# A two-block network on one core: layer norms and residuals of the second block worked one row tile at a time

## The reference, cut to what matters

```python
for layer in range(2):
    mix = even_mixer(x, ...) if layer == 0 else odd_mixer(x, ...)
    x = layer_norm(ALPHA * x + mix, ln1_g, ln1_b)
    x = layer_norm(ALPHA * x + memory_cross_attention(x, mem, xq, xkv, xo), ln2_g, ln2_b)
    x = layer_norm(ALPHA * x + grouped_moe(x, router_w, ...), ln3_g, ln3_b)
```

## Time and profile before

| what | us |
|---|---|
| median of 3 runs | 2657.65 (2654.42 to 2660.9) |
| the profiled execution, its own time | 2666.19 |
| its span, first to last instruction | 2664.3 |
| PE busy | 2455.5 (92%) |
| DVE busy | 1676.5 (63%) |
| ACT busy | 1171.9 (44%) |
| GpSimd busy | 105.5 (4%) |

### The profile page before, as it was taken

How to read it: one execution, slowest core, us unless ns; L and a number is a source line. 1 busy time by engine, 2 the same in 40 slices (tenths; PEclk the granted TensorE clock), 3 DMA queues, 4 the chain that set the end, 5 groups by cost and what they waited for, 6 DMA issues and landing times.

```text
span 2664.3 us, 38999 instructions
## 1 busy us (share of the span) xinstructions
PE 2455.5 (92%) x14431; PEld 2006.1 (75%) x14476; DVE 1676.5 (63%) x2072; ACT 1171.9 (44%) x1418; POOL 105.5 (4%) x76
## 2 busy tenths in 40 slices
PE   8999899999999989999898899989997787999997
PEld 6998787998998878899766778965445666976543
DVE  4666756666666766666544365678875536567776
ACT  5555423444554522444412234456663232446663
POOL 0000140000000022000000000000000000000000
PEclk9999999999999999999998999999998998999998
DMA  6667303665667600566543234678983422568884
GB/s 185 183 186 226 97 1 96 188 183 151 190 188 219 178 10 17 170 182 185 182 136 110 72 119 142 186 272 303 309 311 135 135 71 64 169 210 313 310 308 174
DMA packets 386665, 457.25 MB, mean 172 GB/s; under 512 B 18494, under 2 KB 272994, under 8 KB 386402
## 3 DMA queue, kind: packets, MB, share of 16 engines
q1 hardware_dynamic: 381632, 445.52, 52.4%
q10 hardware_dynamic: 4898, 9.95, 1.2%
HBM read 450.71 MB, written 1.05 MB: 170 GB/s over the span
## 4 chain that ended last, share of the span: by engine, by line
PE 46%; issue 35%; DVE 11%; ACT 3%; POOL 2%; DMA 1%; SPq 0%; ACTq 0%; POOLq 0%; DVEq 0%; PEldq 0%
PE PS L1917 3%; PE PS L1919 3%; PE PS L1918 3%; PE PS L2024 3%; PE PS L2026 2%; PE PS L2025 2%; DVE wlo L1755 2%; PE PS L2117 2%; PE PS L2119 2%; PE PS L2118 2%; PE PS L1934 1%; PE PS L1935 1%; PE PS L1936 1%; ACT whi L782 1%; PE PS L2043 1%
## 5 line engine op out<-in xcount | busy, mean ns | idle before, releaser
L1163 DVE TENSOR_TENSOR wlo<-raw,whi 128x1024 fp32r<-128x1024 f32 x336 | 409.8, 1223 | 308.6 <-ACT whi L735 305.7
L1917 PE MATMUL PS<-xTh,whi 128*128 128x256 f32 x1792 | 508.4, 284 | 4.2 <-DVE xTl L1132 2.2
L735 ACT ACTIVATE whi<-raw 128x1024 fp32r<-128x1024 f32 x336 | 353.9, 1056 | 358.7 <-PE PS L1919 288.7
L1919 PE MATMUL PS<-xTh,wlo 128*128 128x256 f32 x1792 | 507.2, 283 | 0.0
L1918 PE MATMUL PS<-xTl,whi 128*128 128x256 f32 x1792 | 507.2, 283 | 0.0
L1917 PEld LDWEIGHTS PS<-xTh,whi 128*128 128x128 f32 x1792 | 343.5, 192 | 10.5 <-DVE xTl L1132 3.0
L1918 PEld LDWEIGHTS PS<-xTl,whi 128*128 128x128 f32 x1792 | 343.5, 192 | 3.9
L1919 PEld LDWEIGHTS PS<-xTh,wlo 128*128 128x128 f32 x1792 | 343.5, 192 | 0.0
L1755 DVE TENSOR_TENSOR wlo<-raw,whi 128x1024 fp32r<-128x1024 f32 x188 | 222.2, 1218 | 34.1 <-ACT whi L782 33.8
L782 ACT ACTIVATE whi<-raw 128x1024 fp32r<-128x1024 f32 x188 | 190.4, 1051 | 43.5 <-PE PS L2026 21.3
L2117 PE MATMUL PS<-whi,xTh 128*128 128x416 f32 (+2 forms) x480 | 183.9, 383 | 25.8 <-DVE xTl L1132 7.0
(11 more groups left out here) (473 smaller groups left out, 4538.7 us busy)
## 6 DMA issues: line engine op xcount, KB each, us to landing
raw<-in_l_e_gate_dram SPq DMA_DIRECT2D x128, 512.0 KB, 5.1
raw<-in_l_e_up_dram SPq DMA_DIRECT2D x128, 512.0 KB, 6.0
raw<-in_l_e_down_dram SPq DMA_DIRECT2D x128, 512.0 KB, 4.7
raw<-in_ffn_w_gate_dram SPq DMA_DIRECT2D x88, 512.0 KB, 5.3
raw<-in_ffn_w_up_dram SPq DMA_DIRECT2D x88, 512.0 KB, 6.2
raw<-in_ffn_w_down_dram SPq DMA_DIRECT2D x88, 512.0 KB, 3.4
raw<-in_w_in_dram SPq DMA_DIRECT2D x64, 416.0 KB, 4.0
raw<-in_l_xkv_dram SPq DMA_DIRECT2D x32, 512.0 KB, 3.8
```

The lines of the kernel that those rows point to most:

```text
L735: nc.scalar.activation(whi[:, m if slot is None else slot], raw[:, m, j], ACT.Copy).then_inc(hi_done[m], 1)
L1163: nc.vector.tensor_tensor(wlo[:, w], raw[:, m, j], whi[:, w].bitcast(F32), ALU.subtract).then_inc(lo_done[m], 1)
L1917: mm(out_, whi[:, m, ks], xTh[:, k, :], start=(k == 0), stop=False)
L1919: last = mm(out_, wlo[:, m, ks], xTh[:, k, :], start=False, stop=(k == KB - 1))
```

## The change

DVE's norms go tile by tile. `residual` keeps its first half. In the second half (columns 512 to 1023) it takes tile 0 as soon as PE has finished tile 0 of the last chunk (`tile_done`, a signal six matmuls before the group's end), computes the residual and the statistics of that tile, aggregates and asks for its root, then does the same for tile 1 after `group_done`. GpSimd computes a root per tile. `layer_norm` does subtract-and-scale, then root-and-shift, for tile 0, signals `xn_ready`, and then does tile 1. After the experts, the statistics, aggregate and request of a tile follow its own addition.

PE turns `x` with `turn_x`, a tile at a time; `keep_busy(4)` before it becomes `keep_busy(2)`. The wait for all banks in `turned` is gone at turnings 10, 11, 12, 13, 14, 16, 17, 18: the product that follows waits for `xT_dve` bank by bank. Turning 15 keeps it. `turn_for_group` takes the rest of one weight chunk, two banks of `xTl`, the second chunk, and the last two banks. The result is stored in two transfers of 512 KB, one per tile.

```diff
+            for t in range(NT):
+                sp.wait_ge(xn_ready, 2 * LAST_TURN + t + 1)
+                sp.dma_start(out[0, t * P:(t + 1) * P, :], x[:, t]).then_inc(out_done, 16)
...
+            with pool.Fori(0, 3 * DEPTH) as k:
+                for t in range(NT):
+                    rsqrt(RSQ * DEPTH + 2 + 2 * k + t, t, t + 1)
...
+            def ask_tile(t):
+                own(nc.vector.bn_aggr(aggr[:, t], stats[:, t]))
+                nc.vector.tensor_scalar(rs_in[:, t:t + 1], aggr[:, t, 1:2], 1e-5, None, ALU.add).then_inc(rs_asked, 1)
+
+            def layer_norm(k, r):
                 dve.wait_ge(gain_in[0], 16 * (2 + k))
+                dve.wait_ge(gain_in[1], 16 * (1 + k))
                 for t in range(NT):
                     own(nc.vector.scalar_tensor_tensor(out=x[:, t], ... scalar=aggr[:, t, 0:1], in1=gain[:, 0], ...))
-                rsqrt(ask)
-                dve.wait_ge(gain_in[1], 16 * (1 + k))
-                for t in range(NT):
-                    last = nc.vector.scalar_tensor_tensor(out=x[:, t], ... scalar=rs_out[:, t:t + 1], in1=gain[:, 1], ...)
-                last.then_inc(norm_done, 1)
-                dve.wait_ge(norm_done, k + 2)
+                    rsqrt(RSQ * DEPTH + 2 + 2 * k + t)
+                    nc.vector.scalar_tensor_tensor(out=x[:, t], ... scalar=rs_out[:, t:t + 1], in1=gain[:, 1], ...)\
+                        .then_inc(xn_ready, 1)
+                dve.wait_ge(xn_ready, 2 * r + 2)
+                dve.sem_inc(norm_done, 1)
...
+            def turn_for_group(r, width=512, turned=True):
+                if turned:
+                    dve.sem_inc(xn_ready, 2)
+                split_chunks(1, width)
+                turn_split(r, lambda: split_chunks(1, width))
...
+                split_chunks(2)
+                for t in range(NT):
+                    if t == 0:
+                        dve.wait_ge(tile_done, 2 * DEPTH + k + 1)
+                    else:
+                        dve.wait_ge(group_done, n + 2 + CR)
+                    xs = x[:, t, 512:1024]
+                    own(nc.vector.scalar_tensor_tensor(out=xs, in0=xs, scalar=ALPHA, in1=PS[:, 2 + t, :], op0=ALU.mult, op1=ALU.add))
+                    own(nc.vector.bn_stats(stats[:, t, 1], xs))
+                    ask_tile(t)
+                dve.sem_inc(group_out, 1)
...
+                        if tiles and c == 3 and t:
+                            last.then_inc(tile_done, 1)
...
-                keep_busy(4)
-                turn_rows(r, x)
+                keep_busy(2)
+                turn_x(r)
...
+                        if t == 0 and k % 2 == 0:
+                            pe.wait_ge(xT_dve, 4 * (r + 2) + k // 2 + 1)
```

More of the change, by code:

```diff
@@ L141 @@
 SHIFTS = 5
+LAST_TURN = 19
 def both_blocks(nc, A, out):
@@ L1141, in turn_rows, with turn_split @@
                     nc.vector.tensor_copy(dst[:, 2 * b:2 * b + 2, :].rearrange("p k s -> p (k s)"), PS[:, 4 + b, :]).then_inc(xT_dve, 2)
-            def turn_split(r):
+            def turn_split(r, between=None):
                 for b in range(4):
+                    if b == 2 and between:
+                        between()
                     dve.wait_ge(xT_act, 4 * r + b + 1)
@@ L1810, in experts @@
                     own(TTop(x[:, t], x[:, t], acc[:, t * D:(t + 1) * D], ALU.add))
+                    for c in range(2):
+                        last = nc.vector.bn_stats(stats[:, t, c], x[:, t, c * 512:(c + 1) * 512])
+                    own(last)
+                    ask_tile(t)
             split_chunks(2, W0)
@@ L1820, in _ @@
                     turn_for_group(10)
-                    residual(n)
+                    residual(n, 0)
                     r = 11
@@ L2103, in group_end, with group @@
                 pe.sem_inc(group_done, 1)
-            def group(n, n4, ns, slot, width, at=SPLIT_AT, of=(xTh, xTl), r=None):
+            def group(n, n4, ns, slot, width, at=SPLIT_AT, of=(xTh, xTl), r=None, tiles=False):
                 pe.wait_ge(group_out, n + 1)
@@ L2344, in _, with group2 @@
             ns = 10 * DEPTH
-            def group2(n, width, of=(xTh, xTl), r=None):
+            def group2(n, width, of=(xTh, xTl), r=None, tiles=False):
                 nonlocal n4, ns
-                group(n, n4, ns, n % 2, width, of=of, r=r)
+                group(n, n4, ns, n % 2, width, of=of, r=r, tiles=tiles)
                 n4, ns = n4 + 1, ns + 1
@@ L2366, in memory_values, with group_turned @@
                 n4 += 1
-            def group_turned(n, split, of=(xTh, xTl)):
+            def group_turned(n, split, of=(xTh, xTl), r=None):
                 nonlocal n4, ns
@@ L2373, in group_turned @@
                 for c in range(4):
+                    if r is not None:
+                        pe.wait_ge(xT_dve, 4 * r + c + 1)
                     if split:
@@ L2458, in _ @@
                     last.then_inc(pv_psum, 1)
-                    turn_rows(10)
+                    turn_rows(10, wait=False)
                     r = 11
@@ L2520, in _ @@
                     last.then_inc(xT_psum, 1)
-                turned(r + 1)
                 for j in range(2):
-                    group2(n + j, 512)
-                keep_busy(4)
-                turn_rows(r + 2, x)
+                    group2(n + j, 512, r=r + 1 if j == 0 else None, tiles=j == 1)
+                keep_busy(2)
+                turn_x(r + 2)
                 pe.wait_ge(rw_split, 2)
```

65 lines of the change are left out of this document (23 added, 42 removed).

## The result

The changed kernel took 2629.91 us, median of 4 runs (2628.19 to 2633.71); the kernel before, run beside it, 2656.82 (2654.42 to 2660.9, 4 runs). The ratio is 0.9894 with a 95% interval of 0.9876 to 0.9911: 27 us faster. The forecast was 2636.0, with a range of 2626 to 2646. The profiled execution of the changed kernel took 2633.71 us, with a span of 2631.8.

What follows compares the result with a forecast made beforehand. VectorE's own sequence was taken to set the length of the gap at each norm. Gains of 2.4 + 5.8 + 4.7 + 4.9 + 3.1 + 0.7 = 21.6 us off 2657.65 gave 2636.0, range 2626 to 2646.

Steps and rivals of the forecast that it cites:

- The norm: Norms 0, 1, 3, 4: VectorE starts 1.37 us before the old point near E, the group's last matmul end; gain 2.4.
- The root: GpSimd's root per tile: 3.2 and 3.9 us of room for a root of 1.66, so it costs nothing.
- Turning into the product: Norms 0 and 3: from x to the first product matmul 2.3 us instead of 5.16; gain 2.9 each, 5.8.
- rival 3: Late weight loads absorb the turning gain of norms 0, 2 and 3 (8.9 us), giving 2645; chance 0.09.
- The routers: Norms 1 and 4: VectorE's first router instruction comes 2.4 and 2.5 us sooner after x; together 4.9, between 3.5 and 8.
- Turnings 12 and 17: Turnings without a norm: TensorE's idle 2.06 and 1.61 us before the product shrinks to about 0.2; gain 1.9 and 1.4.
- The end: Last norm and store: one 512 KB transfer takes 3.4 us, 1024 KB took 4.0; gain 0.7, between 0 and 2.
- The filler: Halved to 16 zero matmuls, it ends near E + 3.9, before tile 0 is ready at about E + 5; delays nothing.
- the clock: Norms 0 and 3: TensorE's clock still falls to half at the start of the product, as before; no gain counted.
- Rival 1: Clock stays high through the gaps, held by zeros between tiles and shorter idle stretches; gain 30.0, 2627.6 us; chance 0.14.
- Rival 2: Clock falls earlier, during the turning, as transposes don't count as busy work; gain 18.3, 2639.3 us; chance 0.14.
- Rival 4: Halved filler keeps the clock at half through 192 matmuls at norms 0 and 3: 2668 us; 0.06 with other losses.

Runs made afterwards that it cites:

- tiles_only: The changed kernel with the wait for all banks put back and both weight rests ahead of the banks; 2653.84 us, 0.9984 of the kernel before.
- rests_first: The changed kernel with the second weight rest ahead of the bank subtractions instead of between them; 2641.39 us, 0.9928 of the kernel before.
- banks_only: The kernel before with only the bank-by-bank waits and the second rest between the banks, norms left whole; 2637.3 us against 2658.36 beside it.
- early_rest: The changed kernel with one rest moved from behind the norm to before tile 0's residual, at norm 1 the other behind the banks; 2624.96 us.
- second profile: The changed kernel unaltered, run and profiled again; 2633.69 us, 0.9902 of the kernel before.
- roots_four: The changed kernel with three more GpSimd roots ahead of each tile's own; 2643.15 us, one run.
- filler_4: The changed kernel with 32 matmuls of zeros ahead of the four turnings instead of 16; 2636.69 us, 0.9918 of the kernel before.
- no_zeros_between: The changed kernel without the two zero matmuls between the tiles' transposes at norms 0 to 4; 2636.47 us, 0.9908 of the kernel before.
- filler_0: The changed kernel without the filler of zero matmuls ahead of the four turnings; 2630.85 us, 0.9896 of the kernel before.

## Why the forecast was right, term by term

The mechanism was: VectorE's sequence is the gap, and shortening what stands between E and the first bank shortens it one for one. tiles_only (x 0.92 sooner, product 0.93 sooner) and rests_first show it in both directions, banks_only and early_rest where it ends: there TensorE's transposes and ScalarE's first bank take over. The terms, predicted and measured in one profile of either kernel:

| term | predicted | measured | from |
|---|---|---|---|
| norms 0 and 3, norm and turning | 3.5 each | 4.00 each | 13.54 to 9.54 |
| turning 10 | 1.4 | 1.96 | input to first matmul, 6.62 to 4.66 |
| turning 12 | 1.9 | 0.8 | VectorE's first instruction of the attention to first `xo` matmul, 26.37 to 25.59 |
| turning 17 | 1.4 | 2.2 | the same, 27.62 to 25.42 |
| norm 1 and its router | 3.0 | 2.84 | 20.00 to 17.16 |
| norm 4 and its router | 3.1 | 3.27 (1.88 in the second profile) | 17.78 to 14.51 |
| norm 2 | 3.1 | 3.56 | 16.76 to 13.20 |
| end | 0.7 | 1.8 | first addition of the last expert output to the end, 15.76 to 13.94 |
| sum | 21.6 | 24.4 | |
| clock, norms 0 and 3 | 0 | 2.7 + 1.4 (2.7 - 0.1 in the second profile) | product to attention |

That is 28.5; from turning 10 the profiles differ by 30.7, and the medians by 26.9. With the second profile of the changed kernel it is about 26, and 28.4 from turning 10.

- **The norm.** VectorE's head start was 1.44 between the two kernels (E + 0.12 to E - 1.32) where 1.37 was forecast, and from there to x it took 8.78, not 9.0, so that x was ready 0.92 sooner instead of 0.6. At norm 2, where at most 0.2 was forecast, it was 0.45.
- **The root.** Cost nothing, as said. It was even shorter than taken. At norm 0 the second one begins together with a pass of VectorE (1446.04 and 1446.01) and took 0.55; at norms 2 and 5 it begins 0.15 into such a pass and took 1.53, as the 1.66 of the earlier trace rows. So 0.03 into a pass the root was not held up, and 0.15 into it it was. That the cover is 3 us and not endless, roots_four shows.
- **Turning into the product.** 2.9 forecast, 2.93 in banks_only. In the changed kernel x to product is 2.08 us, not 2.3, so 3.1 of gain. Nothing came late in its place: the window from 1454 on shows TensorE busy 2.00 of 2.00, and so does the next, which leaves rival 3 no room.
- **The routers.** From x to the router's first instruction norm 1 took 9.70 us, where 9.2 was forecast from 11.6: a gain of 1.9 and not 2.4, which the larger gain of the norm nearly made up. At norm 4 it took 7.05 for 6.9, but 8.44 in the second profile.
- **Turnings 12 and 17.** The idle time went wholly. At turning 12 the attention's last matmuls before it took 8.86 us instead of 7.17, as 3.4 us of them were at half clock (granted clock 0.81), so 1.1 of the 1.9 did not show.
- **The end** was, with turning 12, the worst-sized term: 0.7 against 1.8. The store gave 1.39, not 0.6, because a load's 3.4 stood in for a store's 2.6, and VectorE 0.43, not 0.1.
- **The filler.** "It delays nothing" was right for half, and filler_4 shows what the whole would have delayed: 0.79 at norms 0 and 3.
- **The step that failed is the clock.** I kept it as before since filler to product would be 6.0 us where it was 6.2 to the fall. Both numbers were off. The product came 5.65 after the filler (1447.57 to 1453.22), as it started at E + 9.54 and not E + 9.9. And the fall of the kernel before was misread: 0.65 over the window 1460 to 1462 is 1.4 us at half clock, so it fell at 1460.6, 5.4 after the filler and 0.8 before the product, not near 1461.3. By its own argument, read rightly, the forecast had still more reason to expect the fall, and it did not come in the first profile. So there is no fixed distance of the kind that the argument needed; the table above shows how far the place varies. Norm 3 was taken to be like norm 0, but its clock had been low for 3.4 us and not 6.8, so only 1.4 was to be had there.
- **The rivals.** Rival 1 came true in part, 4.1 of its 8.4 in the first profile and 2.5 in the second. Of its two reasons the zeros have no part in it at norms 0 and 3; the shorter idle stretches remain. Rival 2 is wrong here for norms 0 and 3. Rival 4, the slower case, was far off: even with no filler the clock was back before the product at norm 0 and 1.0 us into it at norm 3.

So 2629.9 lies 6.1 below the forecast. The kernel before, run beside it, was itself 0.8 faster than the base that the forecast used, so the gain is 5.3 more than forecast. The table gives 6.9 with the first profile (2.8 from terms that were mostly a little small, 4.1 from the clock) and about 4 with the second. That the sum lands so near owes something to luck, as turning 12 and the routers fell short where the norm, turnings 10 and 17 and the end gave more.

## What to carry to other kernels

When several engines pass an operand on in pieces, let the consumer wait for the first piece and order the producer's other work behind it; banks_only got four fifths of this gain with no change in any computation. Then ask who is next: here moving one more instruction out of VectorE's way gave 0.13 of its 1.2, because two other engines needed the same time. And look whether a gap ends near the point at which the clock falls: with 1.1 us more of waiting, in rests_first, the clock fell at both norms and 3.4 and 6.8 us at half clock followed; in the four profiles with 5.5 to 5.6 us from filler to product it fell at two norms of eight.

## What the runs showed of the hardware that I had not expected

- The granted clock came back from 1.2 to 2.4 GHz while TensorE ran nothing but transposes (no_zeros_between, norm 2: from 2017.14, back at 2021.1), whereas sixteen transposes in 3.68 us left it low in the kernel before. With two zero matmuls among the transposes it came back 3.5 us after the first of them in filler_0 at norm 0, and 5.1 us after in the changed kernel at norm 2 (2014.06 to 2019.1).
- A GpSimd root of 128 values took 0.54 to 0.56 us beside VectorE's passes that read PSUM, and beside a pass with two SBUF operands if it began before it or no more than 0.04 us into it. It took 1.2 to 1.5 when it began 0.15 us or more into such a pass; VectorE's own passes kept their 1.28 to 1.30.
- A 512 KB store landed in 2.6 us where loads of 512 KB took 3.4 to 6.2.
- The same code before turning 10 ended up to 14 us apart in profiled executions (1407.2 to 1421.2), as much as most effects studied here; the intervals of norms 0 and 3 repeated to 0.02 us.
